# FFN activations turned by the DMA engines in 16-bit halves in steps 0 to 9 of each FFN, with GpSimd parting and joining the halves

## The reference

```python
def swiglu(x, w_gate, w_up, w_down):
    return (jax.nn.silu(x @ w_gate) * (x @ w_up)) @ w_down

for l in range(DEPTH):                       # DEPTH = 2, SEQ = 256, D_MODEL = 1024, D_FF = 2816
    x = x + 0.5 * swiglu(rmsnorm(x, norm_ffn1[l]), w1_gate[l], w1_up[l], w1_down[l])
    h = rmsnorm(x, norm_mix[l])              # then differential attention and retention on h @ w_in[l]
    x = x + mixed @ w_out[l]
    x = x + 0.5 * swiglu(rmsnorm(x, norm_ffn2[l]), w2_gate[l], w2_up[l], w2_down[l])
return rmsnorm(x, norm_final)
```

## Time and profile before

| | us |
|---|---|
| median of 3 runs | 993.95 |
| lowest and highest | 992.36, 994.07 |
| span of the profiled execution | 992.8 |

### The profile page before, as it was taken

One profiled execution on the slowest core, in us unless ns is written; L12 is line 12 of the kernel. 1 busy time (PEld: TensorE's weight loads), 2 busy tenths in 40 slices (PEclk: granted clock), 3 DMA queues, 4 the chain that ended last, 5 costly groups with the idle time before them and its releaser, 6 DMA issues.

```text
span 992.8 us, 12951 instructions
## 1 busy us (share of the span) xinstructions
PE 965.0 (97%) x4512; PEld 796.2 (80%) x4512; DVE 547.3 (55%) x628; ACT 455.8 (46%) x579; POOL 39.7 (4%) x73
## 2 busy tenths in 40 slices
PE   2999999999999999999999999999999999999997
PEld 2888888888888888888878888888888888888885
DVE  3654545565666645454655545456565755454454
ACT  3634344454573534343453434343655554343432
POOL 3400000000010000000000000000001000000000
PEclk9999999999999999999999999999999999999999
DMA  9664646447245655556536655656634645656541
GB/s 251 219 208 160 208 161 206 171 160 241 91 164 170 205 199 172 208 169 211 188 131 214 188 193 175 205 171 210 209 110 165 213 134 189 212 165 207 164 141 43
DMA packets 123179, 178.70 MB, mean 180 GB/s; under 512 B 5664, under 2 KB 95776, under 8 KB 123136
## 3 DMA queue, kind: packets, MB, share of 16 engines
q1 hardware_dynamic: 121808, 173.56, 52.4%
q0 software_dynamic: 1040, 3.54, 1.5%
q10 hardware_dynamic: 288, 1.05, 0.3%
HBM read 177.08 MB, written 1.05 MB: 179 GB/s over the span
## 4 chain that ended last, share of the span: by engine, by line
PE 95%; DMA 1%; ACT 1%; issue 1%; DVE 1%; SPq 0%; ACTq 0%; POOLq 0%; DVEq 0%; POOL 0%
PE gu L722 20%; PE gu L724 20%; PE gu L723 20%; PE acc L724 10%; PE acc L723 10%; PE acc L722 10%; PE tp L792 2%; DMA raw<-in_w_up_dram 1%; PE tp L737 1%; PE tp L840 1%; PE acc L851 1%; PE tp L863 1%; ACT w_hi L294 0%; ACT wide L394 0%; PE acc L863 0%
## 5 line engine op out<-in xcount | busy, mean ns | idle before, releaser
L478 DVE TENSOR_TENSOR w_lo<-raw,w_hi 128x2048 fp32r<-128x2048 f32 (+1 forms) x168 | 376.2, 2243 | 158.5 <-ACT w_hi L294 158.3
L722 PE MATMUL gu<-w_hi,xT_hi 128*128 128x512 f32 x896 | 353.1, 394 | 11.4 <-DVE w_lo L478 11.0
L724 PE MATMUL gu<-w_hi,xT_lo 128*128 128x512 f32 x896 | 350.2, 391 | 0.0
L723 PE MATMUL gu<-w_lo,xT_hi 128*128 128x512 f32 x896 | 349.7, 390 | 0.0
L294 ACT ACTIVATE w_hi<-raw 128x2048 fp32r<-128x2048 f32 (+1 forms) x168 | 313.8, 1872 | 21.8 <-DMA raw<-in_w_up_dram 11.4
L722 PEld LDWEIGHTS gu<-w_hi,xT_hi 128*128 128x128 f32 x896 | 168.8, 188 | 46.7 <-issue 12.3
L336 ACT ACTIVATE hid<-gu,st 128x256 f32<-128x256 f32 x88 | 41.8, 475 | 352.2 <-PE gu L724 352.1
L724 PEld LDWEIGHTS gu<-w_hi,xT_lo 128*128 128x128 f32 x896 | 168.7, 188 | 35.7
L723 PEld LDWEIGHTS gu<-w_lo,xT_hi 128*128 128x128 f32 x896 | 168.9, 189 | 34.1
L722 PE MATMUL acc<-w_hi,aT_hi 128*128 128x512 f32 x384 | 157.0, 409 | 0.0
L534 DVE SCALAR_TENSOR_TENSOR hid<-gu,st,hid 128x256 f32<-128x256 f32 x88 | 42.5, 483 | 205.3 <-ACT hid L336 205.3
(11 more groups left out here) (111 smaller groups left out, 396.4 us busy)
## 6 DMA issues: line engine op xcount, KB each, us to landing
raw<-in_w_gate_dram SPq DMA_DIRECT2D x88, 512.0 KB, 4.0
raw<-in_w_up_dram SPq DMA_DIRECT2D x88, 512.0 KB, 5.0
raw<-in_w_down_dram SPq DMA_DIRECT2D x88, 512.0 KB, 4.3
raw<-in_w_in_dram SPq DMA_DIRECT2D x40, 512.0 KB, 4.6
raw<-in_w_out_dram SPq DMA_DIRECT2D x16, 512.0 KB, 3.7
raw<-in_w_in_dram SPq DMA_DIRECT2D x16, 256.0 KB, 3.0
gain<-in_norm_ffn_dram POOLq DMA_DIRECT2D x3, 512.0 KB, 4.0
gain<-in_norm_mix_dram POOLq DMA_DIRECT2D x2, 512.0 KB, 4.8
```

Of the source, the lines that this page charges most:

```text
L478: nc.vector.tensor_tensor(w_lo[:, pos % SLOTS, 0:n], raw[:, pos % RAW, 0:n], w_hi[:, pos % SLOTS, 0:n].bitcast(F32), ALU.subtract).then_in ...
L722: nc.tensor.matmul(out_, s_hi, m_hi, start=first, stop=False)
L723: nc.tensor.matmul(out_, s_hi, m_lo, start=False, stop=False)
L724: return nc.tensor.matmul(out_, s_lo, m_hi, start=False, stop=last)
```

## The change

In steps 0 to 9 of each FFN PE no longer turns `hidden`. Instead:

- GpSimd copies `hidden[tt]` (128 x 256 float32) as 16-bit words into `halves`, the 256 low halves first and then the 256 high ones (`turn_out`: 512 words to a partition, read at a stride of two words). It does that once for each token tile.
- ACT waits for both and issues one transposing DMA (`turn`) from `halves` (128 x 1024 words of 16 bits, 256 KB) to `halvesT`.
- GpSimd waits for the DMA and joins the halves back into float32 values in `hidT`, once for each token tile (`turn_back`).
- ACT and DVE make `aT_hi` and `aT_lo` from `hidT` in SBUF instead of `tp` in PSUM (`turned_hi`, `turned_lo`).

ACT's order becomes silu 0, split, silu 1, split, `turn`, `turned_hi` 0, split, `turned_hi` 1. DVE's becomes hide 0, split, hide 1, split, `turned_lo` 0, split, `turned_lo` 1, and each hide from step 1 on also waits until GpSimd has copied the step before. `halves` and `halvesT` lie in `kT`, `hidT` in `qT`. The last step of each FFN stays with PE (`last_hi`, `last_lo`, `hidden_T`). The GpSimd program is unrolled over layers; in the first FFN step 0's parting and joining stand ahead of the constants of the mixer (L247 to L258), and steps 1 to 9 behind them. The order of `up` and `down` on PE, the weights' DMAs and the mixer stay as they are.

The core of the diff:

```diff
+            def turn_out(d, e, tt):
+                pool.wait_ge(hidden_done, e + 1)
+                pool.sem_inc(pool_seen, 1)
+                nc.gpsimd.tensor_copy(halves[:, tt, :, :], hidden[:, tt, :].bitcast(U16).rearrange("p (n h) -> p h n", h=2)).then_inc(halves_done, 1)
+            def turn_back(d, tt):
+                pool.wait_ge(halvesT_loaded, 8 * (d - tt) + 16)
+                pool.sem_inc(pool_seen, 1)
+                nc.gpsimd.tensor_copy(hidT[:, tt, :].bitcast(U16).rearrange("p (n h) -> p h n", h=2), halvesT[:, tt, :, :]).then_inc(hidT_done, 1)
+            def step(d, e, again=True):
+                for tt in range(TT):
+                    turn_out(d + tt, e + tt, tt)
+                for tt in range(TT):
+                    if again:
+                        pool.wait_ge(dT_lo_done, d + tt - 1)
+                    turn_back(d + tt, tt)
...
             for tt in range(TT):
                 entry(0, tt)
+            next_gain(0, norm_mix[0, :])
+            first_steps(0, 0)
             nc.gpsimd.iota(bias8[:, :, :], pattern=[[0, HEADS], [-1, SEQ]], base=P, channel_multiplier=1,
...
+                def turn(d):
+                    act.wait_ge(halves_done, d + 2)
+                    act.sem_inc(halves_seen, 1)
+                    act.dma_start(halvesT.rearrange("p t h (k n) -> p (t h k) n", k=2),
+                                  halves.rearrange("p t h n -> p (t h n)"), transpose=True).then_inc(halvesT_loaded, 16)
...
                     silu(s_, 0, it, pos)
                     nxt(0)
                     silu(s_, 1, it, pos)
-                    hidden_hi(2 * s_, par, 0)
                     nxt(1)
-                    hidden_hi(2 * s_ + 1, par, 1)
+                    turn(d)
+                    turned_hi(d, par, 0)
                     nxt(2)
+                    turned_hi(d + 1, par, 1)
...
-                    hide(e, 0)
+                    hide(e, 0, d - 1 if guard else None)
                     nxt(0)
-                    hide(e + 1, 1)
-                    hidden_lo(e, par, 0)
+                    hide(e + 1, 1, d if guard else None)
                     nxt(1)
-                    hidden_lo(e + 1, par, 1)
+                    turned_lo(d, par, 0)
                     nxt(2)
+                    turned_lo(d + 1, par, 1)
...
                         for tt in range(TT):
-                            hidden_T(e + tt, tt)
-                            down(e - 2 + tt, it, 7 + 3 * u, 1 - u, tt)
+                            down((dT_lo_done, d0 + n - 1 + tt), it, 7 + 3 * u, 1 - u, tt)
```

More of the change, by code:

```diff
@@ L229, in head_factor, with next_gain, first_steps, ffn @@
                 nc.gpsimd.tensor_tensor(h_rstd[:, fs], h_tmp[:, fs], neg_half, ALU.pow).then_inc(done, 1)
+            def next_gain(q, src):
+                pool.wait_ge(xg_ready, 4 * q + 4)
+                load_gain(src)
+            def turn_out(d, e, tt):
[13 more added lines that the diff above has]
+                    turn_back(d + tt, tt)
+            def first_steps(layer, f):
+                i = 2 * layer + f
+                step(2 * (STEPS - 1) * i, 2 * STEPS * i, False)
+            def ffn(layer, f):
+                i = 2 * layer + f
+                d0, e0 = 2 * (STEPS - 1) * i, 2 * STEPS * i
+                with pool.Fori(1, STEPS - 1) as s_:
+                    step(2 * s_ + d0, 2 * s_ + e0)
             nc.gpsimd.memset(ident[:, :], 0.0).then_inc(pool_steps, 1)
@@ L273, in mixer_and_ffn2_entry @@
                     entry(3 * layer + 2, tt)
[L275 to L279, removed]
+            for layer in range(DEPTH):
+                if layer:
                     for tt in range(TT):
@@ L347, in step, with last_step @@
                     silu(s_, 1, it, pos)
-                    hidden_hi(2 * s_, par, 0)
                     nxt(1)
-                    hidden_hi(2 * s_ + 1, par, 1)
+                    turn(d)
+                    turned_hi(d, par, 0)
                     nxt(2)
+                    turned_hi(d + 1, par, 1)
+                def last_step(s_, par, it, pos, nxt):
+                    silu(s_, 0, it, pos)
+                    nxt(0)
+                    silu(s_, 1, it, pos)
+                    last_hi(par, 0)
+                    nxt(1)
+                    last_hi(par, 1)
                 def pieces(it, *lots):
@@ L528, in ffn, with hide, turned_lo, last_lo @@
             def ffn(layer, f, base):
-                e0 = 2 * STEPS * (2 * layer + f)
-                def hide(e, tt):
+                i = 2 * layer + f
+                e0, d0 = 2 * STEPS * i, 2 * (STEPS - 1) * i
+                def hide(e, tt, guard=None):
                     dve.wait_ge(silu_done, e + 1)
+                    if guard is not None:
+                        dve.wait_ge(halves_done, guard)
                     nc.vector.scalar_tensor_tensor(hidden[:, tt, :], gu[tt][:, CH:2 * CH], rstd[:, tt:tt + 1], silu_g[:, tt, :],
                                                    ALU.mult, ALU.mult).then_inc(hidden_done, 1)
-                def hidden_lo(e, par, tt):
-                    dve.wait_ge(hT_hi_done, e + 1)
+                def turned_lo(d, par, tt):
+                    dve.wait_ge(dT_hi_done, d + 1)
+                    ks = slice(2 * par, 2 * par + 2)
+                    lo_of(aT_lo[:, ks, tt * P:(tt + 1) * P], hidT[:, tt, :].rearrange("p (k n) -> p k n", k=2),
+                          aT_hi[:, ks, tt * P:(tt + 1) * P], dT_lo_done)
+                def last_lo(par, tt):
+                    dve.wait_ge(hT_hi_done, 2 * i + tt + 1)
                     ks = slice(2 * par, 2 * par + 2)
@@ L541, in hidden_lo, with step, last_step @@
                           aT_hi[:, ks, tt * P:(tt + 1) * P], hT_lo_done)
-                def step(e, par, it, nxt):
-                    hide(e, 0)
+                def step(e, d, par, it, nxt, guard=True):
+                    hide(e, 0, d - 1 if guard else None)
                     nxt(0)
-                    hide(e + 1, 1)
-                    hidden_lo(e, par, 0)
+                    hide(e + 1, 1, d if guard else None)
                     nxt(1)
-                    hidden_lo(e + 1, par, 1)
+                    turned_lo(d, par, 0)
                     nxt(2)
+                    turned_lo(d + 1, par, 1)
+                def last_step(e, d, par, nxt):
+                    hide(e, 0, d - 1)
+                    nxt(0)
+                    hide(e + 1, 1, d)
+                    last_lo(par, 0)
+                    nxt(1)
+                    last_lo(par, 1)
                 def pieces(it, *lots):
@@ L563, in ffn @@
                 split_lo(layer, base + 2)
-                step(e0, 0, 0, pieces(0, 3, 4, None))
-                step(e0 + 2, 1, 0, pieces(0, 5, 6, 7))
+                step(e0, d0, 0, 0, pieces(0, 3, 4, None), False)
+                step(e0 + 2, d0 + 2, 1, 0, pieces(0, 5, 6, 7))
                 with dve.Fori(0, LOOPED) as it:
@@ L793, in hidden_T, with down @@
                     ins.then_inc(hT_psum, 1)
-                def down(e, it, pos, par, tt, **kw):
-                    pe.wait_ge(hT_lo_done, e + 1)
+                def down(ready, it, pos, par, tt, **kw):
+                    pe.wait_ge(*ready)
                     add_rows(layer, it, tt, base + pos, aT_hi, aT_lo, 2 * par, **kw)
@@ L820, in ffn @@
                         hidden_T(e, 0)
-                    down(e - 2 + tt, 0, p_ + 2, 1, tt)
+                    down((dT_lo_done, d0 + 2 * (STEPS - 1) - 1 + tt), 0, p_ + 2, 1, tt)
                     if tt == 0:
@@ L825, in ffn @@
                         enter_T(q + 1, 0)
-                    down(e + tt, 0, p_ + 3, 0, tt, last=True)
+                    down((hT_lo_done, 2 * i + tt + 1), 0, p_ + 3, 0, tt, last=True)
             def mixer(layer):
```

60 lines of the change are left out of this document (35 added, 25 removed).

## The result

| | before | after |
|---|---|---|
| median, us | 993.44 of 4 runs | 1097.92 of 4 runs |
| lowest and highest | 992.36, 994.07 | 1094.47, 1108.56 |
| profiled execution: its own time, its span | 993.95, 992.8 | 1100.35, 1097.9 |

The change made the kernel slower: the ratio is 1.1069, with a 95% interval of 1.1015 to 1.1122. The time lies 57 us above the upper end of the predicted range.

A forecast was written before the change was run, and what follows sets the result against it. PE's own stream was taken as the bound: 20.0 us saved over 40 steps, 4 lost once in the first FFN, so 976.8 of the profiled 992.8, or 978 beside the median of 993.95; range 972 to 1041.

The forecast's parts named there:

- What bounded the kernel, and what is removed: PE's stream sets the time; dropping two pairs of transposes saves 0.50 us a step, 20.0 us over 40 steps.
- p: One GpSimd copy of 512 words to a partition, parting or joining halves; taken as 0.9 us, between 0.5 and 1.5.
- a rival with 0.10: POOL and DVE hold each other up: copies held 0.75 us each, about 987; chance 0.08, plus 0.02 for more than level.
- X: The 256 KB transposing DMA inside SBUF, from issue on ACT to landing; taken as 4.4 us.
- the ring: DVE's in-order loop through POOL and the DMA, hide 1 to hide 1: 8.8 + 2p + X, 15.0 us, under 16.33.
- the shared 8.7: Large end for X: 64 packets an engine, each turn shared with a weight load, 8.7 us.
- a hidden path: Low end: all 20 us saved, no stand of PE at the start, 974, less 2 for the measurement: 972.
- (2): Second place where the path must fit, DVE's loop: 15.0 us, under 16.33 by 1.3, the tightest of all 40 steps.
- The loop of DVE becomes the bound: Rival: beyond 2p + X = 7.5 the loop sets the step; 1033 at X = 7, 1103 at 8.7; chance 0.30 of slower.
- What would show it: Signs: steps of 16.3 us, DMA landing within 5.5; if over 16.4, waits run PE to DVE to POOL to DMA.
- Once, in the first FFN: GpSimd's 10.1 us of mixer constants between step 0's join and step 1's parting make PE stand about 4 us.
- ACT's and DVE's copies from SBUF: Their two small copies a step read SBUF in place of PSUM; costed at nothing.

The follow-up runs named there:

- the light-load run: Changed kernel with a plain 256 KB copy in 64-byte rows replacing the transposing transfer, weight loads cut to a quarter in most steps: 991.86 us, 0.9988 of before.
- the stand-in: Changed kernel with a plain 256 KB copy in rows of 256 bytes replacing the transposing transfer, nothing turned: 1070.32 us (before: 993.13).

## Why the prediction was wrong

**What bounded the kernel, and what is removed: right.** PE bounded it, and the transposes were worth 0.50 a step and 20.0 us for 40 steps; the run with no transfer gained 19.8 and has steps of 16.33.

**p: right alone, wrong in its place.** The bounds 0.5 to 1.5 hold: 0.62 and 0.75 alone. But in the kernel after the mean parting is 2.28 us. The prediction saw that a parting falls "right onto `nxt(0)`'s `w_lo`", priced it 0.75 by the earlier trace rows, and gave it a rival with 0.10. What those rows show is an iota and selects; the runs here show a copy of SBUF to SBUF that begins behind a `w_lo` lasting until some 0.5 us after that `w_lo` is over, 2.55 us in place of 0.616. The rule of the Trainium skill ("SBUF — State Buffer", Who interferes with whom), which the prediction told and set aside, agrees with that. In the sum it made 10.6 + X into 11.47 + X, 0.87 a step, 35 us. That is less than two `w_lo`, since a parting held by a `w_lo` stands in the ring in place of that `w_lo` and the hide behind it.

**X: the step that failed.** The prediction took 4.4 us, a transfer whose turns are shared with no load; the runs show 7.57, with the loads beside it. The count was right: 40 x 1024 packets are 40960, and q10 has 42528 with all else that it moves. Their price wasn't: 8.1% of 16 x 1097.9 us over 42528 is 33 ns each, not 68. And X was 3.2 where no load ran beside it, below the 4.4 taken: from the turn at 58.48 to the join (the window below; its 82 GB/s are this transfer's 256 KB in 3.21 us), and again at the last turn of all, at 1067.53. A plain copy alone takes 2.97. The Trainium skill ("Advanced Engine Details and Errata", X-Bar Transpose (TRN2)) says that a transposing transfer is as fast as a plain one, and of the transfer alone that holds here.

```profile
58.48:61.69 3.21, 2.43 (x11) 1.69 (x9) 0.00 (x0) 0.00 (x0) 0.00 (x1) 1.00 0.43 82
```

The choice between 4.4 and the shared 8.7 rested on load issues at 113.06 and 118.72, with the turning between them. But those are times of the old order. In the new one the turn waits for a parting, the parting for a `w_lo`, and the same `w_lo` lets SP load: the two are issued together by construction. The median X is 7.57, or 7.84 if it is read from the median distance, 19.31 - 11.47: 3.44 above the value taken. Over 40 steps that is 138 us, with the 35 of the partings 173, less the 53 that the assumed slack of 1.33 holds: 120 above the 972 to 974 of a hidden path. The run has 1098. The shared end, 8.7, was the nearer one.

**The slack of the ring.** "The next steps make up their lateness out of the slack of (2)" counted 1.3 us a step, of a ring on time. Late the ring is 15.9 at X = 4.4, and 16.14 at the 4.67 of the light-load run. That run, with X at 4.3, took 992: even with X as taken, little of the gain would be left. Of its 14 us over the forecast 8.4 are the late third FFN's, and 5 the first one's, which lost 9.1 where 4 were forecast.

**The rival.** "The loop of DVE becomes the bound" is what happened, chain and waits as described under "What would show it". Its own formula at X = 7.84 gives 8.8 + 1.8 + 7.84 = 18.44, 64 + 10 us more than before, 1068; with the 35 us of the held partings, 1103. It had a chance of 0.30, and the range reached only to its X = 7. Of the 126 us against the kernel with no transfer, the 31 distances between turns that follow a turn amid loads (all but each FFN's first and the first FFN's second) hold 89 by their excess over 16.33; the rest lies at the heads and ends of the FFNs, where the last step's PE transposes wait 8.1 us in all for late hides, and I did not split it further.

**Once, in the first FFN.** Forecast 4 us; PE stands 6.16 us there, behind the matmul of 60.52. The order was right; the constants took longer, as they too met `w_lo`. The earlier trace rows has 3.44 for the four multiplies, the kernel after 7.21, and the whole group takes 13.4 us, from 43.87 to 57.26, where it took 10.4. The multiplies doubled for the reason the partings did: two of them take 0.85 us, as before, and the other two begin just behind a `w_lo` (46.59 and 49.19) and take 2.96 (start 46.6) and 2.51 (start 49.7). In the kernel before no `w_lo` ran in their stretch, 25.65 to 29.09.

```profile
43.87 1.00 POOL L291 IOTA bias<- 128x1024 f32 x1
44.97 7.21 POOL L295 TENSOR_SCALAR bias<-bias 128x256 f32<-128x256 f32 x4
56.20 1.06 POOL L301 TENSOR_SCALAR_AFFINE_SELECT decay<-decay 128x1024 f32<-128x1024 f32 x1
```

The ring gets late here, but the second FFN, with no constants in it, is late by its third turn too, as 11.47 + 7.8 is over 16.33 in any case.

**ACT's and DVE's copies from SBUF: right.** 408 and 422 ns against 381 and 416.

## What to carry to other kernels

Before giving work to an engine that waits on a DMA, write the ring of in-order streams it closes, as constant + X, and test it in its late state, with each copy beside the instruction that it will then meet. Price a transfer at the moment it will be issued in the new order, and ask which event releases it and whether the same event releases other transfers. With both neighbours bad, moving the parting to another engine and the split out of the ring was worth 91 us of 1070 in the stand-in, far more than the 20 us the change was after.

## What the chip showed that I had not expected

- A 256 KB transfer inside SBUF whose time alone is 2.97 or 4.1 us landed after 4.3 to 6.7 and 8.2 to 9.9 (medians, by the order of the kernel) beside loads of 1 MB pieces, from a queue of its own that moved 11.54 MB in all. The transposing one took 3.2 and 7.4.
- A GpSimd copy of 512 words of 16 bits, at a stride of two, takes 0.62 us alone, 2.51 to 2.55 when a `w_lo` has just begun. The `w_lo` didn't grow by it at the mean in the kernel after (2292 ns, 2295). Where the copy begins first, the `w_lo` is the longer one: at 35.60, behind a parting of 35.46 that took 0.61, it took 2.61.
- The issue of one transposing transfer takes ACT 1.26 us (L383), that of the plain copy 0.60.
- The part of the ring outside the transfer stays within 11.44 to 11.49 us from step to step in the three kernels that keep the change's order and full loads (after, and the plain copies of 256 and 128 bytes), while X moves by 1 us. With the split first it goes to and fro between 9.5 and 9.7.
